# Attention of a hybrid decoder step: row maxima packed and moved by a step, half of the keys copied by a transfer, output copies issued ahead of the exponentials

## What is computed

```
h = rmsnorm(x)
q, kv_c, kv_s, kv_w, g_nsa, b, c, xs, x_lru, y_lru, g_mix = split(h @ w_in)
o_c, o_s, o_w = compressed, selected and window attention (16 heads, 4 key/value groups, head size 64)
o_nsa = sum of the three, each times its sigmoid gate, per head
u_nsa = o_nsa @ w_nsa_out;  u_sc = short convolution;  u_lru = gated recurrence
x = x + (g0*u_nsa + g1*u_sc + g2*u_lru) @ w_o
x = x + swiglu(rmsnorm(x));  y = rmsnorm(x)
```

## Time and profile before

| | |
|---|---|
| median of three runs | 1171.38 us |
| the profiled execution's own time | 1168.23 us |
| its span, first to last instruction | 1166.5 us |
| TensorE busy | 1121.4 us (96%) |
| VectorE (DVE) busy | 443.7 us (38%) |
| ScalarE (ACT) busy | 372.7 us (32%) |
| GpSimd (POOL) busy | 470.0 us (40%) |
| granted TensorE clock, mean | 0.992 of 2.4 GHz |

### The profile page before, as it was taken

How to read it: one execution, slowest core, us unless ns; L and a number is a source line. 1 busy time by engine, 2 the same in 40 slices (tenths; PEclk the granted TensorE clock), 3 DMA queues, 4 the chain that set the end, 5 groups by cost and what they waited for, 6 DMA issues and landing times.

```text
span 1166.5 us, 20736 instructions
## 1 busy us (share of the span) xinstructions
PE 1121.4 (96%) x8518; PEld 1036.9 (89%) x8518; DVE 443.7 (38%) x625; ACT 372.7 (32%) x497; POOL 470.0 (40%) x265
## 2 busy tenths in 40 slices
PE   6999999999999999899899999999999999999996
PEld 5998999999999988765454599999999999999996
DVE  5847742011211230656672644452332333201142
ACT  6213343232211234245534423342322223221221
POOL 5332545565533414215611134343435343434540
PEclk9999999999999999999999999999999999999998
DMA  8325332323632223542127682323232323222211
GB/s 261 122 72 173 97 89 75 109 68 113 200 108 73 72 77 115 163 137 55 20 56 215 179 306 73 109 73 109 72 108 72 108 75 105 81 91 99 92 54 74
DMA packets 109317, 126.86 MB, mean 109 GB/s; under 512 B 10494, under 2 KB 102806, under 8 KB 107727
## 3 DMA queue, kind: packets, MB, share of 16 engines
q1 hardware_dynamic: 105448, 119.66, 33.0%
q10 hardware_dynamic: 3815, 6.44, 1.7%
HBM read 111.90 MB, written 16.17 MB: 110 GB/s over the span
## 4 chain that ended last, share of the span: by engine, by line
PE 78%; issue 12%; POOL 5%; DVE 3%; ACT 1%; DMA 1%; POOLq 0%; ACTq 0%; DVEq 0%
PE D L1845 57%; PE E L1845 6%; PE D L2084 5%; POOL w_lo L736 5%; PE D L2069 1%; PE D L2070 1%; DVE nmax L1536 1%; PE E L2048 1%; PE E L2140 1%; PE E L2017 1%; PE E L2043 0%; PE E L2100 0%; DVE obuf L1560 0%; PE E L2205 0%; DMA qmx<-th 0%
## 5 line engine op out<-in xcount | busy, mean ns | idle before, releaser
L736 POOL TENSOR_TENSOR w_lo<-w_raw,w_hi 128x1024 fp32r<-128x1024 f32 x164 | 405.2, 2493 | 542.0 <-ACT w_hi L828 522.0
L828 ACT ACTIVATE w_hi<-w_raw 128x1024 fp32r<-128x1024 f32 x164 | 164.2, 1050 | 282.6 <-PE D L1845 239.8
L1845 PE MATMUL D<-hH,w_hi 128*128 128x260 f32 x1152 | 238.8, 289 | 4.5 <-DVE cb L1290 3.2
L1845 PE MATMUL D<-hH,w_lo 128*128 128x260 f32 x1152 | 233.1, 284 | 0.0
L1845 PE MATMUL D<-hL,w_hi 128*128 128x260 f32 x1152 | 232.7, 284 | 0.0
L1845 PEld LDWEIGHTS D<-hH,w_hi 128*128 128x128 f32 x1152 | 179.1, 190 | 9.6 <-issue 5.0
L1845 PEld LDWEIGHTS D<-hH,w_lo 128*128 128x128 f32 x1152 | 178.7, 190 | 0.0
L1845 PEld LDWEIGHTS D<-hL,w_hi 128*128 128x128 f32 x1152 | 178.3, 189 | 0.0
L1845 PE MATMUL D<-onH,w_lo 128*128 128x260 f32 x816 | 164.5, 283 | 0.0
L1845 PE MATMUL D<-onH,w_hi 128*128 128x260 f32 x816 | 164.4, 282 | 0.0
L1845 PE MATMUL D<-onL,w_hi 128*128 128x260 f32 x816 | 164.2, 283 | 0.0
(11 more groups left out here) (375 smaller groups left out, 1456.3 us busy)
## 6 DMA issues: line engine op xcount, KB each, us to landing
w_raw<-in_w_in SPq DMA_DIRECT2D x64, 512.0 KB, 5.0
w_raw<-in_w_ffn_in SPq DMA_DIRECT2D x44, 512.0 KB, 4.4
slot<-in_cache_kv SPq DMA_DIRECT2D x64, 128.0 KB, 2.5
w_raw<-in_w_ffn_out SPq DMA_DIRECT2D x16, 512.0 KB, 3.9
rows_b<-rnorm_d SPq DMA_DIRECT2D x8, 512.0 KB, 5.0
w_raw<-in_w_nsa_out SPq DMA_DIRECT2D x8, 512.0 KB, 6.8
win<-in_cache_win SPq DMA_DIRECT2D x4, 1024.0 KB, 9.2
w_raw<-in_w_o SPq DMA_DIRECT2D x8, 512.0 KB, 4.1
```

The source lines that it names most:

```text
L736: nc.gpsimd.tensor_tensor(wl[b][:, x], raw[b][:, x], wh[b][:, x].bitcast(F32), ALU.subtract)\
L828: nc.scalar.activation(wh[b][:, x], raw[b][:, x], ACT.Copy).then_inc(hi_done, 1)
L1845: ins = mm(out2[:, a, 0:HALF], lhsT, rhs[:, a * HALF:(a + 1) * HALF], start=first, stop=last)
```

## The change

- Group 0's 16 row tiles are laid into the first 13 slots of the last gate chunk (`ROWS_0`: slots 0, 2 and 4 hold two), and the second turn of maxima follows slot 14 instead of the score of step 0. ACT issues both pairs of `max_rows` transfers before its last gate tile; before, the second pair came behind the exponential of step 0.
- The first turn of a group stands behind row tile 8 instead of ahead of it, and on DVE its copy behind the maximum of tile 8.
- For groups 2 and 3 the row tiles lie in steps 6 to 14 of the group before (5 to 14 earlier), for group 1 in steps 8 to 14. The second turn moves from step 15 to 16 and its transfers by a step as well.
- `stage_hi` does three parts instead of four for groups 1 to 3, keys first, then the two halves of the queries; for group 1 behind the exponentials of steps 2, 5 and 7, for the others behind those of steps 0, 1 and 2 of the group before. The fourth part is a transfer within SBUF of 64 partitions by 4 KB (`own_keys`), issued by ACT in step 3 for group 1 and by SP for groups 2 and 3.
- In ACT's loop the output copy of tile t - 4 stands ahead of the exponential of step t.
- The semaphores `x_kept`, `acc_kept` and `th0_kept` become one, `kept`, that counts on; SP waits for the first store before it issues the second.

```diff
...
@@ -464,6 +463,11 @@
                 row = qmx[g % 2][o:o + 1, 2 * a:2 * a + 2, :, :].bitcast(F32).rearrange("o q r x -> o (q r) x")
                 eng.dma_start(row, max_cols(g, a)[br * 8:br * 8 + 8, :]).then_inc(qmx_max[a], 16)
 
+        def own_keys(eng, g):
+            h, o = slice(g % 2 * DH, (g % 2 + 1) * DH), slice((1 - g % 2) * DH, (2 - g % 2) * DH)
+            eng.wait_ge(q_hi, 3 * g + 2)
+            eng.dma_start(k1[g % 2][o, :, :].bitcast(F32), k1[g % 2][h, :, :].bitcast(F32)).then_inc(k_copied, 16)
+
         @block.sync
         def _(sp):
             outs = [0]
...
@@ -534,7 +538,8 @@
             with sp.Fori(0, 2) as i:
                 load_pair(C_Q + 2 * i, COL_Q + i * 2 * CW)
             sp.wait_ge(mixed, 2 + KT)
-            sp.dma_start(acc_d, acc[:, :, :]).then_inc(acc_kept, 16)
+            sp.wait_ge(kept, 16)
+            sp.dma_start(acc_d, acc[:, :, :]).then_inc(kept, 16)
             with sp.Fori(0, 3) as i:
                 load_pair(C_KV + 2 * i, COL_KV + i * 2 * CW)
             with sp.Fori(0, 2) as i:
...
@@ -587,14 +592,14 @@
             rows(1, range(NS))
             for m in range(2):
                 sp.wait_ge(tile_free[m], 1 + C_NSA)
-            sp.dma_start(th0_d, th0[:, :, :]).then_inc(th0_kept, 16)
-            sp.wait_ge(th0_kept, 16)
+            sp.dma_start(th0_d, th0[:, :, :]).then_inc(kept, 16)
+            sp.wait_ge(kept, 48)
             rows(0, range(NS))
             rows(2, range(5))
 
             wk = w_nsa_out[0].rearrange("(kt p) n -> p kt n", p=P)
             def own_q(eng, g):
-                eng.wait_ge(q_hi, 4 * g + 2)
+                eng.wait_ge(q_hi, 3 * g + 4)
                 if g >= 2:
                     eng.wait_ge(scores_done, 2 * NT * (g - 1))
                 h = slice(g % 2 * DH, (g % 2 + 1) * DH)
@@ -603,6 +608,8 @@
             for u in range(2 * GROUPS):
                 if u % 2 == 0 and u // 2 + 1 < GROUPS:
                     own_q(sp, u // 2 + 1)
+                if u % 2 == 1 and u // 2 + 2 < GROUPS:
+                    own_keys(sp, u // 2 + 2)
                 sp.wait_ge(o_evac, 4 * u + 4)
                 sp.dma_start(sums[u % 2][:, :], obuf[u % 2][DH:DH + 1, :, :].rearrange("o r q -> o (r q)"))\
                     .then_inc(sums_landed, 16)
...
@@ -808,9 +815,12 @@
 
             return kT[:, :, :].rearrange("p (br f) t -> p f br t", br=2)[rows, f, :, 0:SEQ]
 
-        def max_step(n):
-
-            return 5 + n * 10 // 16
+        def max_step(g, n):
+
+            return 6 + n * 9 // 16 if g > 1 else 8 + n * 7 // 16
+
+        def stage_step(g, t):
+            return (t - 2 * NT * (g - 1)) if g > 1 else {2: 0, 5: 1, 7: 2}.get(t, 3)
 
         def tiles_through(i):
 
...
@@ -1000,6 +1010,7 @@
             gate_tile(c + 3, 0)
             act.wait_ge(qmx_clear, 4)
             max_rows(act, 0, 0)
+            max_rows(act, 0, 1)
             gate_tile(c + 3, 1)
 
             def on_copy(ft):
@@ -1017,12 +1028,6 @@
                                      accum_out=smalls[:, 1, 0:1]).then_inc(s_exp, 1)
 
             for t in range(STEPS + LAG + 1):
-                if t < STEPS:
-                    act.wait_ge(scores_done, t + 1)
-                    if t >= 4:
-                        act.wait_ge(pv_done, t - 3)
-                    nc.scalar.activation(pT[t % 4][:, :, :].rearrange("p r x -> p (r x)"), D[0][:, t % 2, :], ACT.Exp)\
-                        .then_inc(exp_done, 1)
                 if t > LAG:
                     g, br, qi, kt, i = tile_of(t - LAG - 1)
                     u = i // QT
@@ -1033,16 +1038,22 @@
                         nc.scalar.activation(obuf[u % 2][:, :, qi * P:(qi + 1) * P],
                                              D[1][:, i % 2, :].rearrange("p (r x) -> p r x", r=R), ACT.Copy)\
                             .then_inc(o_evac, 1)
-                if t == 0:
-                    max_rows(act, 0, 1)
+                if t < STEPS:
+                    act.wait_ge(scores_done, t + 1)
+                    if t >= 4:
+                        act.wait_ge(pv_done, t - 3)
+                    nc.scalar.activation(pT[t % 4][:, :, :].rearrange("p r x -> p (r x)"), D[0][:, t % 2, :], ACT.Exp)\
+                        .then_inc(exp_done, 1)
                 if t < LAST and t % (2 * NT) == T_MAX - 3:
                     max_rows(act, t // (2 * NT) + 1, 0)
-                if t < LAST and t % (2 * NT) == T_MAX + 1:
+                if t < LAST and t % (2 * NT) == T_MAX + 2:
                     max_rows(act, t // (2 * NT) + 1, 1)
-                g, n = t // (2 * NT) + 1, t % (2 * NT)
-                if g < GROUPS and 0 <= n < 4:
+                g = t // (2 * NT) + 1
+                if g < GROUPS and stage_step(g, t) < 3:
                     act.wait_ge(scores_done, 2 * NT * (g - 1))
-                    stage_hi(g, n)
+                    stage_hi(g, (stage_step(g, t) + 2) % 3)
+                if t == 3:
+                    own_keys(act, 1)
                 if t == LAST + T_SOFT:
                     soft(0)
                 if LAST + T_ON <= t < LAST + T_ON + 4:
@@ -1510,7 +1521,7 @@
                 b, f, j = g % 2, g // 2, g % 2
                 if n == 3:
                     return
-                dve.wait_ge(q_hi, 4 * g + n + 1)
+                dve.wait_ge(q_hi, n + 1 if g == 0 else 3 * g + 2 + (n + 1) % 3)
                 if n < 2:
                     c = slice(2 * n, 2 * n + 2)
                     q = qT[half(j), 4 * f + 2 * n:4 * f + 2 * n + 2, 0:SEQ].rearrange("p r (q x) -> p q r x", x=P)
@@ -1568,11 +1579,11 @@
                 dst = onT[:, 2 * g:2 * g + 2, :]
                 nc.vector.tensor_tensor(dst, dst, o[:, :, 0, :], ALU.add).then_inc(on_added, 1)
 
-            dve.wait_ge(acc_kept, 16)
+            dve.wait_ge(kept, 32)
             for n in range(16):
                 row_max(n)
-                if n % 8 == 7:
-                    turned_max(0, n // 8)
+                if n in (8, 15):
+                    turned_max(0, n // 15)
             step(nc.vector.tensor_scalar(gate_pk, gate_pk, 1.0, 0.5, ALU.add, ALU.mult))
             dve.wait_ge(cmp_evac, KT)
             def own_queries():
@@ -1656,14 +1667,14 @@
                 if t < STEPS:
                     g, br, qi, kt, i = tile_of(t)
                     if g + 1 < GROUPS:
-                        if 1 <= t % (2 * NT) < 5:
-                            stage_lo(g + 1, t % (2 * NT) - 1)
+                        if t > 0 and 0 <= stage_step(g + 1, t - 1) < 3:
+                            stage_lo(g + 1, (stage_step(g + 1, t - 1) + 2) % 3)
                         for n in range(16):
-                            if max_step(n) == t % (2 * NT):
+                            if max_step(g + 1, n) == t % (2 * NT):
                                 row_max(16 * (g + 1) + n)
-                                if n == 7:
+                                if n == 8:
                                     turned_max(g + 1, 0)
-                        if t % (2 * NT) == T_MAX:
+                        if t % (2 * NT) == T_MAX + 1:
                             turned_max(g + 1, 1)
                 u, n = (t - 16) // NT, (t - 16) % NT
                 if 0 <= u < 2 * GROUPS and n == 0:
@@ -2027,14 +2038,14 @@
                 g, qi, h = n // 16, n % 16 // 4, n % 4
                 b, nk, e = g % 2, (qi + 1) * P, 2 * (n % 2)
                 if n % 16 == 0:
-                    pe.wait_ge(q_hi, 4 * g + 4)
+                    pe.wait_ge(q_hi, 3 * g + 4)
                     pe.wait_ge(q_lo, 3 * g + 3)
+                    if g > 0:
+                        pe.wait_ge(k_copied, 16 * g)
                 if n >= 2:
                     pe.wait_ge(nmax_done, n - 1)
-                if n % 16 == 8:
-                    if g > 0:
-                        pe.wait_ge(nmax_out, 2 * g)
-                    turn_max(g, 0)
+                if n % 16 == 8 and g > 0:
+                    pe.wait_ge(nmax_out, 2 * g)
                 if n % 16 == 9:
                     pe.wait_ge(nmax_out, 2 * g + 1)
                 q = qst[b][:, qi, h, :]
@@ -2049,6 +2060,8 @@
                     for br in range(2):
                         ins = mm(E[:, e + br, qi * P:nk], ident_r[:, :], causal_r[:, :], start=False, stop=True)
                 ins.then_inc(max_mm, 1)
+                if n % 16 == 8:
+                    turn_max(g, 0)
 
             def score_tile(t):
 
@@ -2107,6 +2120,8 @@
                     ins = turn(E[:, 0, q * P:(q + 1) * P], th[:, 1, q * P:(q + 1) * P], ident[:, :])
                 ins.then_inc(pc_turned, 1)
 
+            ROWS_0 = ((0, 1), (2,), (3, 4), (5,), (6, 7), (8,), (9,), (10,), (11,), (12,), (13,), (14,), (15,), (), (), ())
+
             def within(c):
                 def between(m, k):
                     if (c, m) == (C_GM0, 1):
@@ -2123,7 +2138,10 @@
                     if c == C_NSA - 1:
                         if (m, k) == (0, 0):
                             pe.wait_ge(cmp_evac, KT)
```

(24 more changed lines are left out.)

## The result

The kernel after has a median of 1177.70 us in eight runs (1174.65 to 1180.32), the kernel before 1170.45 us beside it in eight, of which the ratio leaves out a slow one of 1377.74 us: ratio 1.0072, 95% interval 1.0060 to 1.0083. That is +0.72%, where the forecast said +0.32%. The kernel got slower, as forecast, and by the mechanism forecast for steps 20 to 59; but the first group got longer where it was forecast to get shorter, and the size was missed. The profiled execution took 1177.75 us, its span 1175.8 us, at a mean granted clock of 0.988 of 2.4 GHz.

A forecast was written before the change was run, and what follows sets the result against it. TensorE, busy 96% of the span, was taken as the bound, losing time to chains. Terms -1.8 + 1.0 + 1.5 - 0.5 + 3.5 = +3.7 us on 1171.38 gave 1175.1 us, range 1168.5 to 1178.5.

The forecast's parts named there:

- Output copy ahead of the exponential: Steps 20 to 59: the copy waiting for add_branch delays exponential and score; +1.0 us in the second stretch, +1.5 in the third.
- The faster rival: Step 24: the copy's wait doesn't hold the exponential, ACT idles under 1 us; -9.2 us, 1162.2 us; chance 0.15.
- The clock in the new gaps: PE's idle stretches before scores 26 and 46 lower its clock; +3.5 us, 1.6 and 1.9.
- the clock stays: Rival: the clock stays at 2.4 GHz in both new gaps; sum +0.2, 1171.6 us; chance 0.17.
- one gap only: Rival: one of the two new gaps is short or costs nothing; sum +2, 1173.4 us; chance 0.15.
- First group, -1.8: Steps 0 to 19: earlier maxima transfers, part of the lead lost to staging; step 20 starts 1.8 us earlier.
- After step 79, 0: From step 79 to the end of the span: no term in the sum, forecast 0.
- Last group, -0.5: Steps 60 to 78: at step 73 the copy no longer stands behind an exponential; -0.5 us.
- Row tiles, turn and staging of groups 2 and 3: Steps 20 to 59: no term of their own, counted within the output copy's +1.0 and +1.5 us.
- Late keys: Rival: the keys' transfer is late for step 8 behind the store; +2 us more, 1177.1 us; chance 0.08.

The follow-up runs named there:

- k4_fill: The changed kernel with 12 matmuls that nobody reads behind the value tiles of steps 25 and 45; 1171.97 us, ratio 1.0021 to the kernel before.
- k1_swap: The changed kernel with the exponential ahead of the output copy again, all else kept; 1168.79 us, ratio 1.0001 to the kernel before.
- k10_add: The changed kernel with add_branch(0) and add_branch(2) ahead of DVE's last low part in steps 23 and 43; 1174.97 us, ratio 1.0041.
- k6_early: k3_cond with group 1 staged in steps 1, 2 and 4 and its row tiles from step 6; 1167.00 us, ratio 0.9984 to the kernel before.
- k5_pool: k3_cond with POOL's clear(1) moved behind the mask of step 2; 1166.02 us, ratio 0.9971 to the kernel before.
- k3_cond: The changed kernel with the output copy behind the exponential only where it waits for add_branch; 1170.03 us, ratio 1.0019 to the kernel before.
- k2_only: The kernel before with only the output copy put ahead of the exponential; 1171.22 us, ratio 1.0020 to the kernel before.
- k9_rows5: The changed kernel with the row tiles of groups 2 and 3 from step 5 again; 1174.10 us, ratio 1.0041 to the kernel before.
- k11_window: k5_pool plus k6_early's staging and row tiles, with the second pair of window loads issued behind branch 6's row sums; 1163.98 us, ratio 0.9952.

## Why the prediction was right or wrong

- **Output copy ahead of the exponential: right.** The score of step 26 stands 11.88 us after that of step 20, before 10.72: +1.16 for the forecast +1.27. For step 46 it is 13.60 for 11.70: +1.90 for +1.35. Without the clock's part (k4_fill: 39.76 and 40.66 us) the two stretches grew by 0.62 and 1.53 us, for +1.0 and +1.5. k1_swap shows that the order on ACT is the cause, k10_add that the addition's end is the gate. The faster rival is dead: ACT's idle time in step 24 is 4.17 us, not under 1.
- **The clock in the new gaps: right, a little small.** It fell after both, 3.22 us and 4.26 us long (forecast 3.9 and 4.4), so "the clock stays" and "one gap only" are dead. k4_fill measures 1.65 and 2.55 us where I took 1.6 and 1.9. The Trainium skill, "TensorE: Matmul & The Clock Gate", section "HAM oscillation - how this bites in real kernels", charges half of the throttled time. As an estimate by that rule, 3.4 us cost 1.7 us and 6.8 us cost 3.4 us. k4_fill bears out the first (1.65, PE was busy for all of it) and not the second: 2.55 was measured, and PE was busy for 5.04 us of 6.5. Half of the busy time, 2.52, is the nearer.
- **First group, -1.8: the failed step, by 2.9 us.** Step 20 starts 1.1 us later than before, not 1.8 earlier. Step 3 did come 3.45 us earlier. I wrote that the lead was lost to staging in step 8 and the crowded steps, and it is (k6_early: 1.75 us). But I had left POOL out of the walk. Its `clear(1)` waits for the last gate matmul, takes until 492.67, and the mask of step 0 stands behind it. Before, this was hidden by the 4.33 us wait for the maxima: with the wait gone, the mask was what came late next, at a price of 3.0 us (k5_pool). With the clearing out of the way step 20 starts 2.0 us earlier than before, about the forecast 1.8, so the rest of the walk held. I had taken it as given that the clock would be 1.00 in steps 3 to 6; it was 0.57 from 493 to 497.
- **After step 79, 0: not in the sum, +2.4 us.** PE's wait for DVE's `kTs` grew by 0.9 us (0.29 before, 1.20 after), and one more low-clock stretch at 667 adds the rest: 3.11 us busy at 0.53 is some 1.5 us more than at 2.4 GHz (an estimate). The tail differs between kernels whose code behind step 79 is the same (525.45 us in k1_swap, 524.45 in k3_cond, 524.44 in k4_fill), so part of this is the execution and not the change; the eight runs (1174.65 us at 0.990 to 1180.32 at 0.984) go with their clock. It isn't settled by a run of its own.
- **Last group, -0.5: right.** Steps 60 to 78 took 0.52 us less, and 36.81 us instead of 36.34 with the exponential ahead again (k1_swap).
- **Row tiles, turn and staging of groups 2 and 3:** right in sign and undervalued by being counted with the copies. Without the copies' edit the two stretches are 1.27 us and 0.55 us shorter than before (k1_swap 37.87 and 38.58 for 39.14 and 39.13); the three were not tried apart. This gain is lost with the copies' edit, so that the order on ACT costs 3.3 us at score 26 in the new layout (11.88 for 8.57), where I counted only the 1.27 against the kernel before. But they also took the only work out of step 25 that lay inside the idle time; k2_only and k9_rows5 show that this is what made one long piece of it.
- **Late keys:** dead, 2.9 and 4.9 us.

The range (1168.5 to 1178.5) held the 1177.7 us, near its top; the two failed terms, +2.9 and +2.4 us, are nearly all that lies between the sum and the 9.3 us of the profiled executions. The joined semaphore and the keys' transfer were not tried by themselves.

## What to carry to other kernels

Before you put a short operation ahead of the one that feeds the busiest engine, look at every wait it can have: on an in-order engine its worst wait becomes the wait of all that stands behind it (here 4.2 and 5.2 us of it, against 0.5 us saved in the last group). When a wait of several microseconds goes, walk all five engines through the same microseconds to find what was late under its cover; here it was a memset. And before you move small work out of an idle stretch of TensorE, ask what the stretch will be without it: with such work in it the clock stayed at 1.00 in k4_fill and k9_rows5, though not in k2_only.

## What the runs showed of the hardware that I had not expected

- Idle time of PE in two pieces of 2.72 and 0.82 us (k9_rows5), or one of 2.10 (k10_add), left the clock at 1.00; 3.01, 3.22 and 4.26 us in one piece were followed by 0.50 to 0.52. But so were, at 1.2 GHz as well, 1.92 and 2.22 us (k2_only) and 1.17 and 1.43 us with 1.3 us between them (after, score 2 and value tile 0). The length of the idle time alone doesn't tell which it will be.
- The same waits can give either clock: k11_window has the waits of k3_cond in the same places of the third stretch (1.02 and 1.27 us, for 1.02 and 1.28), and yet 0.58 from 574.5 to 578.5, at a cost of 1.6 us (40.19 for 38.57); k3_cond kept 1.00. What decides there stays open.

```profile
574.50:578.50 4.00, 3.91 (x11) 2.48 (x11) 1.28 (x4) 2.01 (x4) 0.63 (x1) 0.58 0.04 6
```

- Twelve matmuls whose results nobody reads, laid into each of the two idle times of PE, kept the clock at 1.00 behind them and took 4.2 us off the two stretches; the kernel's ratio fell from 1.0072 to 1.0021, part of it (1.95 us of the profiled executions) behind step 79, which the edit doesn't touch.
